# Two expert passes fewer, the final stage laid under the last four passes, and a gate product moved ahead of compress

## What is computed

```python
h = rmsnorm(x, norm1_g); z = h @ w_in
y_ssm = s5_mixer(z[..., :512]) # diagonal state space, GELU, then ya * sigmoid(yb), [ya, yb] = y @ w_glu
y_attn = nsa_mixer(...)        # compressed, selected and window branches; the first needs compress()
x = x + concat(y_ssm, y_attn) @ w_out
h = rmsnorm(x, norm2_g)
x = x + hier_moe(h)            # 4 groups of 8 experts: top-1 group, top-2 experts inside it
out = rmsnorm(x, final_g)      # the final stage
```

## Time and profile before

| | |
|---|---|
| median of three runs | 1125.66 us (1124.25 to 1126.36) |
| the profiled execution, its own time | 1124.31 us |
| its span (first to last instruction) | 1122.4 us |
| mean granted clock of PE | 0.954 |
| PE busy | 1015.0 us, 90% |
| DVE, ACT, POOL busy | 495.0, 274.6, 161.3 us |
| DMA | 163.16 MB, mean 145 GB/s |

### The profile page before, as it was taken

One profiled execution on the slowest core, in us unless ns is written; L12 is line 12 of the kernel. 1 busy time (PEld: TensorE's weight loads), 2 busy tenths in 40 slices (PEclk: granted clock), 3 DMA queues, 4 the chain that ended last, 5 costly groups with the idle time before them and its releaser, 6 DMA issues. The chain is left out here.

```text
span 1122.4 us, 13494 instructions
## 1 busy us (share of the span) xinstructions
PE 1015.0 (90%) x5111; PEld 597.1 (53%) x5111; DVE 495.0 (44%) x1214; ACT 274.6 (24%) x629; POOL 161.3 (14%) x150
## 2 busy tenths in 40 slices
PE   6999999975599989999999999996999999979980
PEld 4434777764455456666667455563554444434430
DVE  3477560068815466665665124274721211212214
ACT  3200110130112377566655011120101110101113
POOL 3000000025301131201010000011212122111210
PEclk9999999986899999999999999987999999989995
DMA  9200020032400091000000243455889999999728
GB/s 257 90 19 25 1 76 0 1 43 75 96 1 1 1 256 52 2 1 2 1 2 2 75 150 125 193 218 226 270 305 361 378 390 390 378 367 363 271 49 306
DMA packets 53632, 163.16 MB, mean 145 GB/s; under 512 B 24759, under 2 KB 26871, under 8 KB 41207
## 3 DMA queue, kind: packets, MB, share of 16 engines
q1 hardware_dynamic: 45184, 144.38, 35.8%
q0 software_dynamic: 8384, 17.91, 6.5%
HBM read 145.28 MB, written 26.29 MB: 153 GB/s over the span
## 5 line engine op out<-in xcount | busy, mean ns | idle before, releaser
L1885 PE MATMUL banks<-shared,wout 128*128 128x512 f32 (+1 forms) x416 | 159.4, 612 | 11.3 <-issue 9.6
L1539 PE MATMUL banks<-wout,shared 128*128 128x512 f32 x256 | 112.7, 594 | 0.5 <-PEq L1202 0.5
L364 PE MATMUL banks<-x,wout 128*128 128x512 f32 x256 | 112.0, 594 | 1.1 <-DVE x L405 1.1
L1885 PEld LDWEIGHTS banks<-shared,wout 128*128 128x128 f32 (+1 forms) x416 | 62.6, 175 | 87.9 <-issue 87.7
L1250 ACT ACTIVATE shared<-shared,low 128x640 f32<-128x640 f32 (+7 forms) x128 | 92.9, 729 | 2.6 <-DVE low L1337 2.1
L1933 DVE SCALAR_TENSOR_TENSOR mix_bt<-mix_bt,slot_coef,banks 128x256 f32<-128x256 f32 x26 | 12.5, 480 | 174.0 <-ACT mix_bt L1913 173.9
L1300 PE MATMUL banks<-consts,shared 128*128 128x128 f32 x528 | 77.8, 282 | 4.4 <-ACT shared L1250 3.6
L1907 PE MATMUL banks<-shared,hidt 128*128 128x512 f32 (+1 forms) x208 | 79.6, 595 | 0.8 <-ACT hidt L1917 0.8
L364 PEld LDWEIGHTS banks<-x,wout 128*128 128x128 f32 x256 | 47.8, 190 | 60.2 <-issue 58.1
L1300 PEld LDWEIGHTS banks<-consts,shared 128*128 128x128 f32 x528 | 56.0, 140 | 43.8 <-issue 38.2
L1866 POOL DMA_INDIRECT x_rows<-wout,tok x26 | 41.4, 1593 | 255.2 <-DVE wout L1940 236.5
(11 more groups left out here) (349 smaller groups left out, 1289.6 us busy)
## 6 DMA issues: line engine op xcount, KB each, us to landing
shared<-in_exp_w_down SPq DMA_DIRECT2D x26, 1024.0 KB, 21.1
shared<-in_exp_w_gate SPq DMA_DIRECT2D x26, 1024.0 KB, 10.7
shared<-in_exp_w_up SPq DMA_DIRECT2D x26, 1024.0 KB, 21.3
x<-in_exp_w_gate SPq DMA_DIRECT2D x6, 1024.0 KB, 13.6
x<-in_exp_w_up SPq DMA_DIRECT2D x6, 1024.0 KB, 23.4
x<-in_exp_w_down SPq DMA_DIRECT2D x6, 1024.0 KB, 22.2
shared<-in_x SPq DMA_DIRECT2D x8, 512.0 KB, 7.6
wout<-in_w_in SPq DMA_DIRECT2D x2, 2048.0 KB, 8.5
```

The lines of the kernel that those rows point to most:

```text
L364: ins = nc.tensor.matmul(bank[:], slot[:, c, c0:c0 + P], ht[:, c, half * 512:half * 512 + 512], **flags)
L1539: ins = nc.tensor.matmul(psum[n % 4], src[:, i * P:i * P + P], m["wout"][:, k, half * 512:half * 512 + 512], start=k == 0, stop=k == KD - 1)
L1885: ins = nc.tensor.matmul(psum[2 + p][rows].rearrange("p (a f) -> p a f", a=2), xt[:, p, k, rows], wgu[b][:, :, k], start=k == 0, stop=k == ...
```

## The change

1. `FULL` becomes 5: 10 singles and 8 pairs, 24 passes. The string of passes changes, with pairs earlier. The table `EXPERT` renumbers the experts, so that the halves are the groups 0 and 2 and the groups 1 and 3; routing (`pick`), the fixed experts, the list of ids and the list of overflows follow it. The sum of weight loads stays at 32 experts.
2. The last four passes (20 to 23, all singles, `DIRECT` = 4) no longer scatter. When scatter 19 has landed, SP loads the eight tiles of `x_rows`; ACT, DVE and SP square, scale and store them between the steps of passes 21 to 23. For the four passes POOL gathers the rows' residuals from `x_rows` (`residual_rows`), DVE adds them to the down product in PSUM (`dve_sum`, all 1,024 columns), ACT and DVE normalise the sum, and POOL writes these rows straight to the output (`put_out`), over what the tiles left there. The sums of passes 20 and 21 are also written to `x_rows` (`put_rows`), because a row of pass 22 or 23 can stand in them too. All of the final stage is done once more behind the overflow loop if that runs (`all_again`).
3. In compress, PE does `glu(0, 1)` and `glu(0, 0)` before the transpose of the positions, and ACT the tanh of it (`gate(0)`) before the three negated copies.

```diff
-RANKED, FULL = E // 2 - 3, 7
+RANKED, FULL = E // 2 - 3, 5
+EXPERT = [2 * EPG * (n % (2 * EPG) // EPG) + EPG * (n // (2 * EPG)) + n % EPG for n in range(E)]
+DIRECT = 4
...
+            pe.wait_ge(m["wglu_in"], 16)
+            for part in (1, 0):
+                glu(0, part)
             pe.wait_ge(pos_in, 16 * (KV + 2))
...
-            pe.wait_ge(m["wglu_in"], 16)
-            for part in (1, 0):
-                glu(0, part)
             pe.wait_ge(m["w1_in"], 16 * 4)
...
-    order = statics + [(singles if kind == "S" else pairs).pop(0) for kind in "PSSPSSPSSPSSPSSPSSSS"]
+    order = statics + [(singles if kind == "S" else pairs).pop(0) for kind in "PSPSPPSPSPPSPSSSSS"]
...
+    def residual_rows(gp, n):
+        rows_landed(gp, max(first - 1, n - 2))
+        gp.wait_ge(s["x_t"], 2 * n + 2)
+        nc.gpsimd.indirect_dma_start(xg[:, n % UN], None, m["x_rows"],
+                                     bass.IndirectOffsetOnAxis(m["tok"][:, passes[n][0]:passes[n][0] + 1], 0),
...
+    def put_rows(gp, n):
+        gp.wait_ge(s["y_act"], n + 1)
+        gp.wait_ge(s["y_dve"], n + 1)
...
+    def put_out(gp, i):
+        n = first + i
+        gp.wait_ge(o_done, nth_norm["z", i])
+        gp.wait_ge(out_stored, 16 * NT)
+        if i == 2:
+            for k in range(2):
+                out_landed(gp, k)
+        nc.gpsimd.indirect_dma_start(out[0], bass.IndirectOffsetOnAxis(m["tok"][:, passes[n][0]:passes[n][0] + 1], 0),
...
+    def dve_sum(dve, n):
+        dve.wait_ge(s["y_done"], n + 1)
+        dve.wait_ge(x_in[n % UN], 16 * gathered[n] + 16)
+        dve.wait_ge(stored[n % 2], rows_out(n))
+        if n - 2 >= first:
+            dve.wait_ge(o_done, nth_norm["z", n - 2 - first])
+        for part, done in enumerate(("y_act", "y_dve")):
+            cols = slice(part * 512, part * 512 + 512)
+            V.tensor_tensor(y[:, n % 2, cols], xg[:, n % UN, cols], psum[6 + part], ALU.add).then_inc(s[done], 1)
...
+            rows_landed(sp, first - 1)
             for i in range(NT):
-                sp.dma_start(m["x1"][:, i], last_rows[i]).then_inc(last_in[i][0], 16)
+                sp.dma_start(homes[i], last_rows[i]).then_inc(last_in[i][0], 16)
             for i in range(NT):
-                sp.wait_ge(o_done, i + 1)
-                sp.dma_start(out_rows[i], m["x1"][:, i]).then_inc(out_stored, 16)
+                sp.wait_ge(o_done, nth_norm["x", i])
+                sp.dma_start(out_rows[i], homes[i]).then_inc(out_stored, 16)
             sp.wait_ge(out_stored, 16 * NT)
+            for i in range(DIRECT):
+                out_landed(sp, i)
...
+                if n == first + 1:
+                    residual_rows(gp, first)
+                    residual_rows(gp, n)
+                    for i in range(NT):
+                        gp.wait_ge(*last_in[i])
+                    put_rows(gp, first)
+                elif n == first + 2:
+                    put_rows(gp, n - 1)
+                    residual_rows(gp, n)
+                elif n > first:
+                    residual_rows(gp, n)
+            for i in range(DIRECT):
+                put_out(gp, i)
```

More of the change, by code:

```diff
@@ L1853, in stage_moe @@
     over_w = 1 + max(nth[j] for j in range(len(loads)) if buffer_of(j) == 0)
-    over_x = 1 + max(gathered[n] for n in range(0, NP, UN))
+    over_x = 3 + max(gathered[n] for n in range(0, NP, UN))
     over_st = (NP + 1) // 2
+    first = NP - DIRECT
+    assert buffer_of(passes[first - 1][1][-1]) == 0
+    assert all(buffer_of(j) for n in range(first, NP) for j in passes[n][1])
+    assert not any(passes[n][2] & passes[n - 1][2] for n in range(first, NP) if n > first)
+    homes = ([wgu[0].rearrange("p a k f -> p (a k f)")[:, i * D:i * D + D] for i in range(4)]
+             + [wd[0][:, i] for i in range(2)] + [m["spare"][:, i * D:i * D + D] for i in range(2)])
+    by_square = [("z", 0)] + [("x", i) for i in range(4)] + [("x", i) for i in range(4, NT)] + [("z", i) for i in range(1, DIRECT)]
+    by_norm = [("x", i) for i in range(4)] + [("z", 0)] + [("x", i) for i in range(4, NT)] + [("z", i) for i in range(1, DIRECT)]
+    groups = [slice(0, 5), slice(5, 10), slice(10, 11), slice(11, 12)]
+    nth_norm = {what: k + 1 for k, what in enumerate(by_norm)}
+    column = {what: slice(k, k + 1) for k, what in enumerate(by_square)}
     def gather(n):
@@ L2219, in some, with inverses @@
                     next(parts, None)
+            def inverses(g):
+                dve.wait_ge(root_done, g + 1)
+                inverse_root(nc, chain, rstd[:, groups[g]], root[:, groups[g]], ss[:, groups[g]], newton)
             dve_x(dve, 0, 0)
@@ L2236, in _ @@
                     some(5)
-            dve_y(dve, NP - 1, (NP - 1) % 2, rows_out(NP - 1))
+            dve_sum(dve, NP - 1)
+            for i in range(2, DIRECT):
+                inverses(i)
+                dve_scaled(("z", i))
             def over_tile(k):
```

151 lines of the change are left out of this document (109 added, 42 removed).

## The result

| | before | after |
|---|---|---|
| median of the runs, us | 1126.01 (1124.25 to 1128.27, 4 runs) | 1113.76 (1112.53 to 1115.26, 4 runs) |
| ratio to before, 95% interval | 1 | 0.9884 (0.9864 to 0.9903) |
| profiled execution and its span, us | 1124.3, 1122.4 | 1113.3, 1111.4 |
| TensorE busy, us | 1015.0 | 1002.5 |
| DMA moved, MB | 163.16 | 164.89 |

The change is faster by 1.2%, some 12 us between the medians and 11.0 between the two spans. The forecast was 5.8 us, for the span as for the median. The direction came as forecast; the gain was about twice the forecast one. First, the rows of the changed kernel that answer to those of before.

What follows compares the result with a forecast made beforehand. It took the DMA queue to bound the expert stage: tiles in at 1079.2 plus a 40.6 us tail, less 3.4 (gate unit), plus 0.2 (routing), gave span 1116.6, 5.8 under before; forecast 1119.9 us, range 1114 to 1123.

Steps and rivals of the forecast that it cites:

- Both resources full, the queue the later one: Mid expert stage: TensorE and DMA both full, with the queue already later for a while, by 9 us in all.
- Only the rows of two passes come through, 2 x 3.7 = 7.4 us: Expert stage: of 22.8 us saved on TensorE only 7.4 come through, with the last weights at 1069.4.
- Rival 1: Expert stage: the queue never runs dry, the pairs removing all 13 us of idle queue; 1107 us, chance 0.12.
- The tiles in 9.8 us behind the weights: Start of the tail: eight tile loads queue behind the last weights and are all in 9.8 us later, at 1079.2.
- Waits at the low clock cost nothing while loads are outstanding: Expert stage: slow products (9.86 against 6.87 us) hide behind outstanding loads, so the sum counts one for pass 23 alone.
- rival 4: Expert stage: TensorE's low-clock waits cost 3 us each and the queue runs dry; two leave 1126 us, chance 0.15.
- ScalarE as the cover that fails: Tail: ScalarE's tile squares delay passes 22 and 23, with the sum of pass 22 from about 12.5 us after the last tile.
- The chain through GpSimd: Tail: row writes, gather, sum, scalings, stores and output writes in series, 6.0 us per row write, 40.6 us after the last tile.
- rival 2: Tail: short links, each row transfer 3.5 us in place of 6, four giving back 10; 1110 us, chance 0.06.
- rival 3: Tail: row transfers at full-queue prices of 10.0 and 11.8 us, 15.7 us more; 1136 us, chance 0.15.
- The gate unit, 3.4 us: Start of compress: gate products fill TensorE's idle hole and bring 3.4 us, bounds 1.5 and 4.5.
- The old tail for a new one nearly as long: End of the kernel: 7.4 us of queue and 31.7 us of old tail buy a new tail nearly as long.

Runs made afterwards that it cites:

- e6: The changed kernel with only half of each gate and up weight loaded: 1079.1 us, ratio 0.9584.
- e13: The kernel before with only the order of its passes changed, its six paired passes early: 1127.01 us, ratio 1.000.
- e3: The changed kernel with 26 passes (FULL 7, the old string), keeping new halves, new tail and gate unit ahead: 1119.58 us, ratio 0.993.
- e9: The changed kernel with four filler products on TensorE ahead of the weight waits of passes 13, 15, 16 and 18: 1114.04 us, ratio 0.988.
- e10: The changed kernel with the row writes of the last four passes, to x_rows and to the output, made accumulating: 1122.22 us, ratio 0.9958.
- e5: The changed kernel with ScalarE's tile squares behind all activations and all tile scalings ahead of the sum of pass 22: 1122.53 us, ratio 0.9968.
- e1: The changed kernel with the gate unit put back behind the flips in compress: 1116.97 us, ratio 0.9909.
- e2: The kernel before with the 24 passes alone (new halves, new order), old final stage and compress: 1118.38 us, ratio 0.9916.
- e11: The changed kernel with the scatters of passes 0 to 19 writing without adding: 1095.76 us, ratio 0.9717.
- e12: The changed kernel with two activations ahead of the squares, own PSUM banks for pass 23, tiles scaled before pass 22's sum: 1109.67 us, ratio 0.985.

## Why the prediction was half right

Two terms of the sum were mis-sized: the 7.4 us for the rows of two passes (point 2) and the 6.0 us for each row write of the tail (point 6). The missed 5.2 us split at T, the landing of the last tile, without a rest: T came at 1074.2, not 1076.0 (1.8 us), and from T to the end of the span it took 37.2 us, not 40.6 (3.4 us). T is where the prediction counts from, and not a point of the measured chain: that goes through the fourth tile (1069.2), ScalarE, TensorE's pass 23 and the sum of pass 22 (point 5).

1. *Both resources full, the queue the later one.* Right. The waits came where they were foretold, ahead of paired passes. They are shorter than the "5 us and more" of the text and begin at pass 11, not 13; e6 shows what they wait for.

2. *Only the rows of two passes come through, 2 x 3.7 = 7.4 us.* **This term was mis-sized.** The last weights landed 13.6 us earlier, of which the gate unit's 3.4 come off: 10.2. The price of a pass holds: between the same landings, 18 experts apart, the queue took 189.4 us with 15 scatters and gathers before (57.1 / 15 = 3.8 a pass) and 178.0 with 13 after (3.5). (These are the passes whose scatter and gather landed in between.) So 11.4 us of queue time went, 4 more than the rows of two passes, and the 178.0 comes again in the other traces with the change's passes (177.0 to 178.4), while the 189.4 is of the one trace of before. What was probably missing is the other effect of a string with its pairs early: more loads stand in the queue sooner, so it runs dry less. e13, which has this and no fewer passes, puts it at 2.8 us by its last landing and at 1.7 to 4.5 by its queue time. That 7.4 + 2.8 is just 10.2 is luck: e3, with neither fewer passes nor the new order, has its last weights at 1070.7, 6.1 us ahead of those of the kernel before, of which the earlier start (first reload of down weights at 787.8 and not 792.6) explains 4.8. Rival 1 named this mechanism, found 13 us of idle queue and argued that nothing would change there; some of them went, two to five by these figures.

3. *The tiles in 9.8 us behind the weights.* 11.0 measured. With 3.0 us from the weights (13.6 against 10.6 with the gate unit's share) that makes the 1.8.

4. *Waits at the low clock cost nothing while loads are outstanding.* Right, by e9's queue. The products behind four of the waits took 8.6 to 9.8 us, so rival 4 had its condition several times over, and not its price. That price was 1.6 to 2.8 us for each and not 3, since the 6.87 us set against 9.86 are those of a single pass, and a paired product takes 7.02 at the full clock. The Trainium skill, "TensorE: Matmul & The Clock Gate", section "HAM oscillation — how this bites in real kernels", describes waits for data that throttle the engine again and again; the trace agrees that they do, and by e9 it isn't paid for here.

5. *ScalarE as the cover that fails.* Right: it squares tiles from 1065.45 on, TensorE idles 6.80 us behind it, and pass 23's product takes 9.49 us. I judged this path (sum of pass 22 at T + 12.5) to be hidden by the gather at T + 15. It came to T + 14.3 and the gather to T + 13.0, so TensorE's path was the later one, by 1.3 us.

6. *The chain through GpSimd.* **The links were mis-sized.** The rows of the tail:

| step | forecast, after T | measured, after T |
|---|---|---|
| write of pass 20 landed | 6.0 | 4.6 (issued at 1.0, 3.6 long) |
| residual rows of pass 22 in | 15 | 13.0 |
| sum of pass 22 starts | 15 | 14.3 |
| last tile scaled | 20.0 | 19.2 |
| last tile stored | 24.0 | 22.0 (2.8 long) |
| first pair of output writes landed | 31.9 | 29.3 |
| second pair landed | 39.8 | 34.7 |
| end | 40.6 | 37.2 |

Of the 3.4 us the two pairs of output writes have 3.1 (7.3 and 5.4 us for 7.9 each), the store of the last tile 1.2 and the earlier sum 0.8; the end took back 1.7. The shorter first write is not among them, since TensorE's path hid it.

The step that failed is the choice of 6.02, the price of before's last scatter, for writes that don't accumulate. That row is, by my count of the routing, a pass of 52 rows, fewer than any of the new writes carries (55 to 73), with little else in the queue, so the count of rows could not be the reason for its length; the adding was, and e10 shows it by putting it back: 6.1 us for the first write, 8.3 us on the whole. e10 shows something else: with links of the priced kind the tail took 47.2 us from T (1121.4 - 1074.2), 6.6 more than the 40.6 of the sum. So the sum came as near as 3.4 us partly by luck: its writes were too dear, and against adding writes of up to 7.5 us, issues of GpSimd of 1.5 to 2.7 us, and 2.5 us at the end it was too cheap. I had this as rival 2 at a chance of 0.06, against it the argument that a gather without adding also takes 5.98. That argument compared a read with a write, and its row isn't the price of an idle queue: the gather at 761.32 ran beside the weights that landed at 766.0 and three more gathers. In the tail the gathers took 8.2 to 8.5 us beside the stores, but in e5, where no store ran beside it, the gather for pass 22 took 4.2. The Trainium skill, "DMA: Bandwidth & Descriptors", section "Anatomy of one DMA — SWDGE (gpsimd) path", gives 3.2 us for 0.5 MB by its fit, and for the 0.2 to 0.3 MB of 55 to 73 rows an estimate of 2.5 to 2.7. The trace is 0.5 to 1 us above that for plain row writes with nothing beside them (3.2 to 3.6), and far above it for adding ones (6.1 and more) and for the gathers beside stores. The rival of full-queue prices (rival 3, 1136 us) fell: behind T no link came near 10 us.

One item went the other way: from the last landing (1108.9) to the end of the span are 2.5 us, not 0.8.

7. *The gate unit, 3.4 us.* The transposes, windows and all behind them start 3.3 us earlier, the expert stage 3.6; e1 gives 2.4 of span and 2.8 of time, and the starts of the expert stage in all traces 3.2. Right. The clock rose with the work, 0.95 from 305 to 310 and not 0.61.

8. *The old tail for a new one nearly as long.* Right in its sense and sharper than I had it: on top of the fewer passes the new tail brings under 1 us (e2 against e1). Of the whole gain of 12 to 13 us, the fewer passes have about 9 and the gate unit 3.

Open: how much of the queue's idle time the fewer passes removed and how much their order did, beyond the one comparison of e13. That would need the string of e13 and that of the change at several numbers of passes, which was not tried.

## What to carry to other kernels

Price a transfer by its kind: a row write that accumulates costs more, both alone and in the queue, than a plain one, and a scatter's price can't be taken for a write that only looks like it. Where the queue is the bound, look for work to take out of it before taking work off the engine; here dropping the adding would have been worth more than the whole change, if the algorithm allowed it. And before a block is moved off one engine's path, ask what runs under it for free: e5 lost 9 us by moving ten squares out from under the landings and a product. And if the pieces of a sum add up, that doesn't show that each is right: here links priced too high stood beside issues priced too low.

## What the runs showed that was not expected

- An accumulating row write of 0.3 MB or less: 6.1 to 7.5 us to landing on a nearly idle queue, a plain one 3.2 to 4.7 (e10 against the changed kernel); in a full queue 1.2 us more of queue time each (e11), and 1.56 against 1.00 us of GpSimd to issue.
- A plain row write beside tile stores takes as long as an accumulating one alone: 6.0 and 6.9 us in e12, against 3.6 and 3.2 in the changed kernel, whose stores start 3.7 us behind the first of them. The gathers show the same: 8.2 and 8.5 us beside stores in the changed kernel, 4.2 with none beside it in e5, 4.7 behind the first four in e12. VectorE was scaling at the same times; with scaling and no store, at 1097.01 in the changed kernel, a plain write took 4.7 us, 1.1 of it a longer issue, so the scaling isn't the larger part of the 6.0 and 6.9.
- GpSimd's issue of a row transfer took 1.95 and 2.07 us at 1079.01 and 1097.01 in the changed kernel, where VectorE was scaling 1,024 columns at the time, and 0.97 at 1104.31, when VectorE was done. It isn't a rule: at 1077.35 the issue took 0.99 us though VectorE began to scale at 1077.58, and at 1083.48 in e12 it took 1.02 us in the midst of scalings. Why wasn't tried.
- TensorE ran paired products at 8.6 to 9.8 us and not 7.0 behind waits of 3.1 to 4.5 us, but at 7.09 behind a wait of 3.52 us at 1003.68: the wait's length alone doesn't tell which.
